# A state-space layer inside a two-block network: within-chunk blocks multiplied in four quadrants and placed by transfers, skip term by TensorE, decay rows by ScalarE

## What is computed

```python
def s5_mixer(h, a_re, a_im, log_dt, b_re, b_im, c_re, c_im, d_skip, w_glu):
    ...                      # ab = exp(a * dt), bb = discretised b, complex
    u = h.reshape(B, S, S5_GROUPS, S5_GROUP)          # 128 groups of 16 channels
    def per_sequence(u_s):
        bu_re = jnp.einsum('sgc,gpc->sgp', u_s, bb_re)
        bu_im = jnp.einsum('sgc,gpc->sgp', u_s, bb_im)
        _, _, x_re, x_im = lax.associative_scan(_scan_combine, (a_seq_re, a_seq_im, bu_re, bu_im), axis=0)
        return jnp.einsum('sgp,gcp->sgc', x_re, cr) - jnp.einsum('sgp,gcp->sgc', x_im, ci)
    y = lax.map(per_sequence, u).reshape(B, S, D)
    y = y + d_skip * h                                # the skip term
    g = jax.nn.gelu(y)
    val, gate = jnp.split(g @ w_glu, 2, axis=-1)
    return val * jax.nn.sigmoid(gate)
```

## Time and profile before

| | us |
|---|---|
| median of 3 runs (2895.97 to 2900.55) | 2896.2 |
| span of the profiled execution, first to last instruction | 2892.0 |
| TensorE busy (19064 matmuls) | 2857.4 |
| VectorE busy | 1879.2 |
| ScalarE busy | 1417.9 |
| GpSimd busy | 393.4 |
| the S5 loop, first `drive` to the first product of `gl0` | 1884.4 to 2000.1 |
| one turn of the loop, by the starts of `drive` | 7.30 |

### The profile page before, as it was taken

One profiled execution on the slowest core, in us unless ns is written; L12 is line 12 of the kernel. 1 busy time (PEld: TensorE's weight loads), 2 busy tenths in 40 slices (PEclk: granted clock), 3 DMA queues, 4 the chain that ended last, 5 costly groups with the idle time before them and its releaser, 6 DMA issues.

```text
span 2892.0 us, 45428 instructions
## 1 busy us (share of the span) xinstructions
PE 2857.4 (99%) x19064; PEld 2606.1 (90%) x19064; DVE 1879.2 (65%) x2575; ACT 1417.9 (49%) x1964; POOL 393.4 (14%) x444
## 2 busy tenths in 40 slices
PE   8999999999999999999999999999999999999998
PEld 8999988998899988989998899898889999988997
DVE  6998655766566655778666666588555555555555
ACT  5445645456455555444444445654545444444444
POOL 0000000000000000008873663043000000000000
PEclk9999999999999999999999999999999999999999
DMA  7555455552555545567776666585655555555553
GB/s 244 190 195 172 155 189 187 188 178 74 187 195 172 171 168 175 193 202 248 238 245 216 231 230 211 186 258 165 204 190 184 195 191 194 198 190 192 197 194 131
DMA packets 288043, 558.45 MB, mean 193 GB/s; under 512 B 27424, under 2 KB 35872, under 8 KB 287584
## 3 DMA queue, kind: packets, MB, share of 16 engines
q1 hardware_dynamic: 281376, 531.27, 55.7%
q0 software_dynamic: 5456, 21.73, 1.9%
q10 hardware_dynamic: 1008, 2.55, 0.3%
HBM read 530.34 MB, written 25.17 MB: 192 GB/s over the span
## 4 chain that ended last, share of the span: by engine, by line
PE 92%; DVE 4%; ACT 2%; issue 1%; POOL 0%; DMA 0%; ACTq 0%; DVEq 0%; POOLq 0%
PE G L506 86%; PE T L506 4%; DVE WL L1648 1%; ACT WH L1071 1%; DVE Y L1656 1%; PE T L585 1%; PE G L979 0%; ACT SC_e L1074 0%; DVE X L1648 0%; DVE ST L1729 0%; DVE SC_e L1656 0%; ACT L1068 0%; POOL ZZ L2428 0%; DMA X<-in_x 0%; PE T L964 0%
## 5 line engine op out<-in xcount | busy, mean ns | idle before, releaser
L1648 DVE TENSOR_TENSOR WL<-RAW,WH 128x1024 fp32r<-128x1024 f32 (+1 forms) x948 | 1183.8, 1258 | 754.7 <-ACT WH L1071 745.3
L1071 ACT ACTIVATE WH<-RAW 128x1024 fp32r<-128x1024 f32 (+1 forms) x948 | 993.8, 1055 | 1027.4 <-PE G L506 1025.5
L506 PE MATMUL G<-A1h,WH 128*128 128x256 f32 (+1 forms) x2583 | 717.9, 279 | 1.6 <-DVE WL L1648 1.6
L506 PE MATMUL G<-A1l,WH 128*128 128x256 f32 x2560 | 710.7, 278 | 0.0
L506 PE MATMUL G<-A1h,WL 128*128 128x256 f32 x2560 | 709.4, 277 | 0.0
L506 PEld LDWEIGHTS G<-A1h,WH 128*128 128x128 f32 x2583 | 485.7, 188 | 5.1 <-DVE WL L1648 2.9
L506 PEld LDWEIGHTS G<-A1l,WH 128*128 128x128 f32 x2560 | 482.3, 188 | 0.4
L506 PEld LDWEIGHTS G<-A1h,WL 128*128 128x128 f32 x2560 | 482.4, 188 | 0.0
L506 PE MATMUL G<-WH,Bh 128*128 128x512 f32 x1024 | 399.3, 390 | 0.6 <-DVE WL L1648 0.6
L506 PE MATMUL G<-WH,Bl 128*128 128x512 f32 x1024 | 398.5, 389 | 0.0
L506 PE MATMUL G<-WL,Bh 128*128 128x512 f32 x1024 | 398.5, 389 | 0.0
(11 more groups left out here) (325 smaller groups left out, 3564.6 us busy)
## 6 DMA issues: line engine op xcount, KB each, us to landing
RAW<-in_mlp_w SPq DMA_DIRECT2D x256, 1024.0 KB, 5.4
RAW<-in_even_w_in SPq DMA_DIRECT2D x52, 1024.0 KB, 5.0
RAW<-in_a_w_in SPq DMA_DIRECT2D x48, 1024.0 KB, 5.2
RAW<-in_b_w_glu SPq DMA_DIRECT2D x32, 1024.0 KB, 5.4
RAW<-in_odd_w_in SPq DMA_DIRECT2D x20, 1024.0 KB, 5.0
RAW<-in_even_w_out SPq DMA_DIRECT2D x16, 1024.0 KB, 5.1
RAW<-in_odd_w_out SPq DMA_DIRECT2D x16, 1024.0 KB, 5.1
RAW<-in_a_w_out SPq DMA_DIRECT2D x16, 1024.0 KB, 5.0
```

What stands on the lines that cost most here:

```text
L506: return e.matmul(out, lhsT, rhs, start=start, stop=stop, skip_group_check=True)
L1071: return e.activation(out, in_, ACT.Copy, scale=scale, bias=0.0)
L1648: return e.tensor_tensor(out, a, b, op)
```

## The change

Five things are changed in the S5 stage.

1. `within` puts the four pairs on the four partition quarters of the bank (rows 32m to 32m+31, columns 0 to 127) and takes the products in another order (i outside, m inside). Four products of 32x32, of the identity with a new matrix DD, add the diagonal of d to the first 32 columns: the skip term is now part of the block.
2. `within` (ACT) makes one copy of 128x128 into KD. SP writes KD to a DRAM tensor (`blocks_out`, 64 KB) and, when that has landed, reads it into FD with four transfers (`blocks_placed`, 64, 48, 32 and 16 KB), which do the shift. `feed` waits for these.
3. `feed` moves one turn later on PE, and behind `within`: the loop is `drive(a)`, `turn_w(a+1)`, `within(a+1)`, `feed(a-1)`, `readout(a-1)`; `feed(15)` and `readout(15)` go into `gl0`.
4. `output` (DVE) is gone, as are DU (POOL) and DST; gelu reads the PSUM bank.
5. The decay rows MG are made by ACT (`decay`, four copies of 128x64 with a scale) instead of by POOL (one product of 128x256).

```diff
@@ pe @@
+            if a == 0:
+                e.wait_ge(*eye["d"])
+            for i in range(2):
+                for m in range(4):
+                    mm(T[32 * m:32 * m + 32, 0:128], W[:, i, m, 96:128], R[:, i, m, 0:128], i == 0, False)
             for m in range(4):
-                for i in range(2):
-                    tk = mm(T[0:32, 128 * m:128 * m + 128], W[:, i, m, 96:128], R[:, i, m, 0:128], i == 0, i == 1)
+                tk = mm(T[32 * m:32 * m + 32, 0:32], IDENT[:, 32 * m:32 * m + 32], DD[:, a, :], False, True)
             tk.then_inc(*f_mm.up(a))
...
         def feed(a):
-            e.wait_ge(*f_c[a])
+            e.wait_ge(*k_back[a % 2][a])
             if a >= 2:
-                e.wait_ge(*y_sum[a - 2])
+                e.wait_ge(*gelu[a - 2])
...
             if 1 <= a < 15:
                 turn_w(a + 1)
-            feed(a)
-            if 1 <= a < 15:
                 within(a + 1)
             if a:
+                feed(a - 1)
                 readout(a - 1)
+        def last_readout():
+            feed(15)
+            readout(15)
@@ act @@
             if a >= 2:
-                e.wait_ge(*fd_mm[a - 2])
-            elif a == 0:
-                e.wait_ge(*zeros["fd"])
-            T = block_bank(a)[0:32, :].rearrange("p (a b) -> p a b", b=128)
-            for j in range(4):
-                c = copy(FD[a % 2][32 * j:32 * j + 32, :, 32 * j:128], T[:, :, 0:128 - 32 * j])
-            c.then_inc(*f_c.up(a))
+                e.wait_ge(*k_out[a % 2][a - 2])
+            copy(KD[a % 2], block_bank(a)[:, 0:128]).then_inc(*f_c.up(a))
+
+        def decay(a):
+            if a >= 2:
+                e.wait_ge(*scan[a - 2])
+            for m in range(4):
+                d = copy(MG[a % 2][:, 64 * m:64 * m + 64], KEEP[:, :], M4[:, 4 * a + m:4 * a + m + 1])
+            d.then_inc(*mg.up(a))
...
-            fn(YG[a % 2], YS[a % 2], ACT.Gelu_apprx_tanh).then_inc(*gelu.up(a))
+            fn(YG[a % 2], G[a % 2][:, 0:256], ACT.Gelu_apprx_tanh).then_inc(*gelu.up(a))
@@ dve @@
-        def output(a):
-            e.wait_ge(*y_mm[a])
-            e.wait_ge(*du[a])
-            if a >= 2:
-                e.wait_ge(*gelu[a - 2])
-            tt(YS[a % 2], G[a % 2][:, 0:256], DU[a % 2], ALU.add).then_inc(*y_sum.up(a))
@@ pool @@
+        tt(DD, EYE.unsqueeze(1).to_broadcast([128, 16, 32]), col("b_d", 0, 16).unsqueeze(2).to_broadcast([128, 16, 32]),
+           ALU.mult).then_inc(*eye.up("d"))
...
-            tt(by_pair(DU[a % 2]), US[:, m, :], DST[:, m].unsqueeze(2).to_broadcast([128, 4, 64]), ALU.mult).then_inc(*du.up(a))
-            if a >= 2:
-                e.wait_ge(*scan[a - 2])
-            tt(MG[a % 2].rearrange("p (a b) -> p a b", b=64), KEEP[:, :].unsqueeze(1).to_broadcast([128, 4, 64]),
-               M4[:, m].unsqueeze(2).to_broadcast([128, 4, 64]), ALU.mult).then_inc(*mg.up(a))
@@ sp @@
+        def blocks_out(a):
+            e.wait_ge(*f_c[a])
+            e.dma_start(KR[a], KD[a % 2]).then_inc(*k_out[a % 2].up(a, 16))
+
+        def blocks_placed(a):
+            e.wait_ge(*k_out[a % 2][a])
+            if a >= 2:
+                e.wait_ge(*fd_mm[a - 2])
+            else:
+                e.wait_ge(*zeros["fd"])
+            v = KR[a].rearrange("(m c) x -> c m x", c=32)
+            for j in range(4):
+                e.dma_start(FD[a % 2][32 * j:32 * j + 32, :, 32 * j:128], v[:, :, 0:128 - 32 * j]).then_inc(
+                    *k_back[a % 2].up(a, 16))
...
             for a in range(20):
+                if 2 <= a < 16:
+                    blocks_placed(a)
                 if a < 14:
                     drive_matrices(a + 2)
                 if a == 0:
                     stacks(3)
+                    blocks_out(0)
+                    blocks_out(1)
+                if a == 1:
+                    blocks_placed(0)
+                    blocks_placed(1)
...
                 if 3 <= a < 19:
                     gelu_out(a - 3)
+                if 1 <= a < 15:
+                    blocks_out(a + 1)
                 if a in (3, 5, 7, 9):
                     load(gl0 + (a - 3) // 2)
```

More of the change, by code:

```diff
@@ L206, in build_program @@
     M4 = sb("M4", [128, 64], ctx=ctxs)
-    DST = sb("DST", [128, 64], ctx=ctxs)
+    sb("pad_dst", [128, 64], ctx=ctxs)
     RBS = sb("RBS", [128, 64], ctx=ctxs)
@@ L222, in build_program @@
     CTD = [VAR5[:, 2048 + 256 * i:2304 + 256 * i].rearrange("p (a b) -> p a b", b=16) for i in range(2)]
-    YS, DU, MG, YG = ([VAR5[:, 512 * n + 256 * i:512 * n + 256 * i + 256] for i in range(2)] for n in range(4))
+    MG, YG = ([VAR5[:, 512 * n + 256 * i:512 * n + 256 * i + 256] for i in range(2)] for n in (2, 3))
+    DD = VAR5[:, 0:512].rearrange("p (a b) -> p a b", b=32)
+    KD = [VAR5[:, 512 + 128 * i:640 + 128 * i] for i in range(2)]
+    EYE = VAR5[:, 768:800]
     YB = [VAR5[:, 2048 + 256 * i:2304 + 256 * i] for i in range(4)]
@@ L234, in build_program @@
     HD = nc.dram_tensor("s5_h", (4, 128, 4, 256), F32, kind="Internal").ap()
+    KR = nc.dram_tensor("s5_k", (16, 128, 128), F32, kind="Internal").ap()
     YD = nc.dram_tensor("s5_y", (16, 4, 32, 4, 64), F32, kind="Internal").ap()
@@ L413, in build_program @@
     u_sc = sig("u_sc")
-    du = sig("du")
+    eye = sig("eye")
+    k_out = [sig(f"k_out{i}") for i in range(2)]
+    k_back = [sig(f"k_back{i}") for i in range(2)]
     mg = sig("mg")
@@ L425, in build_program @@
     y_mm = sig("y_mm")
-    y_sum = sig("y_sum")
     gelu = sig("gelu")
@@ L453, in taken @@
         if tag == "s5_y":
-            return y_sum[14 + i]
+            return gelu[14 + i]
         if tag == "s5_w":
@@ L1045, in pe @@
             gemm(f"gl{i}", A1h, A1l, None if i else (lambda kt: e.wait_ge(*g_low[kt])),
-                 None if i else (lambda: readout(15)), 1)
+                 None if i else last_readout, 1)
             gemm(f"gg{i}", A1h, A1l)
@@ L1565, in act @@
         mlp(0, "s", HT, lambda k: col("norm_mix", 16 + k), first_matrices)
+        e.wait_ge(*zeros["keep"])
+        e.wait_ge(*d_step["m4"])
+        decay(0)
         turned(1)
@@ L1568, in act @@
         for a in range(16):
+            if a < 15:
+                decay(a + 1)
             if a >= 2:
@@ L1584, in act @@
         high_tile(11)
-        e.wait_ge(*fd_mm[15])
+        e.wait_ge(*y_mm[14])
         for _ in range(RS - 2):
@@ L2280, in s5_params @@
             yield
-            for m in range(4):
-                for j in range(4):
-                    e.tensor_copy(DST[32 * j:32 * j + 32, m:64:4], col("b_d", 0, 16)[32 * m:32 * m + 32, :]).then_inc(
-                        *d_step.up("dst"))
-                    yield
         def params():
@@ L2340, in dve @@
         for a in range(16):
-            if a >= 2:
-                output(a - 2)
             chain(a)
@@ L2348, in dve @@
                 low_tile(a - 5)
-        output(14)
         low_tile(11)
@@ L2354, in dve @@
         low_tile(12)
-        output(15)
         low_tile(13)
@@ L2500, in pool @@
             e.dma_start(SPR[a], STR).then_inc(*sp_r.up(a, 16))
+        for m in range(4):
+            if m:
+                e.wait_ge(*eye[m - 1])
+                tt(EYE, EYE, IDENT[:, 32 * m:32 * m + 32], ALU.add).then_inc(*eye.up(m))
+            else:
+                e.tensor_copy(EYE, IDENT[:, 0:32]).then_inc(*eye.up(m))
+        e.wait_ge(*eye[3])
+        tt(DD, EYE.unsqueeze(1).to_broadcast([128, 16, 32]), col("b_d", 0, 16).unsqueeze(2).to_broadcast([128, 16, 32]),
+           ALU.mult).then_inc(*eye.up("d"))
         e.wait_ge(*c_io["c"])
```

6 lines of the change are left out of this document (1 added, 5 removed).

## The result

The changed kernel takes 2925.6 us in the median (2922.5 to 2928.7), the kernel before 2898.4 us beside it on the same chip (2896.0 to 2902.4). The ratio is 1.0094, 95% interval 1.0082 to 1.0105. It is slower, as forecast, and SP's stream sets the pace of the loop, as forecast. But it loses 27 us where 9.6 were worked out, and the time lies above the range of 2892 to 2919. A trace is of one execution, which can be some us from the median of its kernel (this one took 2928.7 us).

The account below looks back on a forecast made before the run. TensorE bounds the kernel before at 7.30 us a turn; after, SP's stream would at 8.8. A loop 8.7 us longer plus 0.9 for `feed(15)` gives +9.6 on the 2896.2 median: 2906 us, range 2892 to 2919.

Parts of the forecast that it names:

- the main case: S5 loop: SP's turn of 8.3 to 9.6 us, L from 3.1 to 4.4, time 2901 to 2914; chance 0.55.
- the sum's own terms: SP's turn from WB to WB: 3.13 + 3.6 + 1.89 + 0.2 = 8.8 us.
- L: In SP's stream, time from issuing `blocks_out` to its landing: taken as 3.6 us, ends 1.6 and 5.6.
- the walk: Step-by-step times through the S5 stage: WB(4) at 1901.1, WB(6) 1916.0, WB(15) 1995.2, `gl0` at 2008.8.
- then `blocks_out(3)` when the copy is there, near 1902: Start of the stage: `blocks_out(3)` issued near 1902, landing 3.6 us later at 1905.6, WB(5) at 1907.6.
- some 5 us: Start of the stage: TensorE stands still for some 5 us before `feed(0)`.
- the sentence on the clock: End of the stage: the kernel before's clock loss there is left as it is, despite TensorE waiting some 2.6 us each turn.
- The short round trip: Rival in SP's loop: `blocks_out` lands at L = 2.0 or less, turn 7.2 us, about 2889 us; chance 0.15.
- The quarters do overlap: Against the rival in `within` of no overlap: up to 2.8 us instead of 0.8, time 2908; chance 0.08.
- The rival of the clock: Rival in the loop: waits bring TensorE to 1.2 GHz for part of every turn, turn 9.3 us, 2914; chance 0.17.
- ScalarE's decay copies cost nothing: Loop: ACT's decay copies ahead of `turned`, which might hold `drive`, priced at nothing because `scan[a-1]` is done earlier.

Follow-up runs that it names:

- the run with the filled wait: Changed kernel plus twelve unread identity products (36 in the first turn) between `drive` and `turn_w`, to hold TensorE's clock up; 2928.1 us, ratio 1.0109.
- the transfer by ScalarE: Changed kernel with `blocks_out` issued by ScalarE right behind its copy to KD, placements still by SP; 2908.3 us, ratio 1.0040.
- RD behind: Changed kernel with the load of the readout matrices (RD) issued behind the blocks' transfer to `s_k`, not ahead of it; 2922.2 us, ratio 1.0079.
- both orders: Changed kernel with placements issued behind the four GELU-tile writes and the RD load behind the blocks' transfer to `s_k`; 2912.4 us, ratio 1.0045.

## Why the prediction was right in kind and wrong in size

**TensorE's part was right.** 6.2 us a turn forecast, 6.12 measured; `within` and the identity 0.8, measured 0.46 + 0.18 = 0.64.

**That SP's stream would bound the loop was right**, and the place of the wait too. The turn was 9.69 us instead of 8.8, just above the 9.6 at which the main case ended. Over the nine turns from WB(6) to WB(15), by the sum's own terms:

| term | forecast | measured (mean) |
|---|---|---|
| WB, RD, read and four writes, to `blocks_out` | 3.13 | 3.72 |
| L, `blocks_out` to its landing | 3.6 | 3.91 |
| placements, to the next WB | 1.89 | 2.06 |
| the 1 MB load | 0.2 | 0, it lies inside L |

The term most mis-sized is the first, the issues: I had taken their price from single turns of the kernel before. In the changed loop four writes take 1.85 to 2.81 us (2.13 in the turn above) and four placements up to 2.76. I take it that the queue accepts more slowly when more is under way; no run isolates that. 9 x 0.89 = 8.0 us. L was a good guess, though by rows that did not quite say it: the 3.4 us of the earlier trace rows is the median of all 61 writes, not of those behind a RD load. In the nine turns L is 2.5 to 5.3. In the three turns that hold a 1 MB load it is 2.5 to 3.5 and the turn some 9 us; in the turn behind each of them it is 4.4 to 5.3 and the turn some 11. The last two turns alternate in the same way without a load (8.46 and 9.89), so the load is not all of it.

**The start was wrong by 6 us**: WB(6) at 1921.98, not 1916.0. Up to WB(4) the walk holds (1901.1 forecast, 1901.65 measured). The step that failed is the next, "then `blocks_out(3)` when the copy is there, near 1902". It came at 1909.48, and SP waited 6.1 us for the copy. TensorE shows why:

```profile
1897.66 1.97 PE L511 MATMUL G<-US,FD 128*128 128x64 f32 x8 [7.85 <-DMA FD<-s_k]
1899.42 3.62 PE L511 MATMUL G<-ZZ,RD 128*128 128x63 f32 x16
1902.84 3.62 PE L511 MATMUL T<-US,LAM 128*128 128x64 f32 x16
1906.25 1.91 PE L984 MATMUL G<-CID,WB 128*128 128x128 f32 x8
1908.09 0.90 PE L511 MATMUL T<-RD,WB 128*32 128x128 f32 x16
```

I had forecast "some 5 us" of standing still; it was 7.85. And behind it the clock was at half: from this `feed` to `within` 1908.09 - 1897.66 = 10.4 us, where the same four steps take 0.94 + 1.79 + 1.79 + 0.97 = 5.5 in the turn shown first. These 5 us are nearly all of the six. I had followed SP's stream to 1902 and not the chain on TensorE that the copy hangs on: even at full clock `within` would have started at 1903.2 and `blocks_out(3)` near 1904.5. That the rest would be won back at full clock is read from these rows and from the run with the filled wait (5.5 us there too, without its filler), which made the start longer by other means. A shorter wait alone does not do it: without the long wait (the first block's round trip moved before the start), and without any transfer, the same steps took 10.4 and 10.5 us.

**The end was wrong by 7 us**: 20.6 us from WB(15) to `gl0`, not 13.6.

```profile
2013.03 1.09 PE L984 MATMUL G<-CID,WB 128*128 128x128 f32 x8 [1.95 <-DMA WB<-s_w]
2014.99 1.08 PE L511 MATMUL T<-RD,WB 128*32 128x128 f32 x16 [0.87 <-issue]
...
2017.88 3.62 PE L511 MATMUL G<-ZZ,RD 128*128 128x63 f32 x16
2021.29 3.62 PE L511 MATMUL T<-US,WT 128*128 128x64 f32 x16
```

At full clock it is 13.7 (the run with the filled wait), which is the forecast. The step that failed is the sentence on the clock: "I leave this loss in the end of the stage as it is". The rows at 1992 had shown the loss for a short stretch; here everything behind the last `turn_w` runs at half speed: 14.8 us from `within` (2014.99) to `gl0`, where it is 7.9 in the run with the filled wait (2016.40 to 2024.27).

**Sum**: forecast 8.7, start 6.0, turns 8.0, end 7.0: 29.7 us, and `gl0` begins at 2029.79 instead of 2000.06, 29.7 later. `feed(15)` inside `gl0` and a longer stretch at half clock there add 2.1 (0.9 forecast). The profiled executions are 34.8 us apart. The last 3 us come behind a wait of 2.78 us for DVE that both have, some 185 us after the start of `gl0`: in the changed kernel it is followed by half clock, in the kernel before by full clock. As far as the traces tell this does not belong to the change: in three more kernels with the same code from there on (the transfer by ScalarE, RD behind, both orders) the mean clock of the 20 us around this wait was 0.91, 1.00 and 0.91, where it is 0.83 and 1.00 in the two compared. The medians are only 27.2 apart, since the trace of the changed kernel is of an execution above its median (2928.7 us, 2925.6) and that of the kernel before of one below its median (a span of 2892.0; 2898.4). So the account is one of the two traces; for the medians it is 7.6 us too long, and no trace says which of its terms are smaller there.

**The rivals.** The short round trip did not come: L was 3.9, not 2.0. The quarters do overlap. The rival of the clock happened, but together with the main case and in another place than I had put it. I had weighed it only by whether TensorE's turn would pass SP's; in the loop it did not matter (9.61 and 9.69). It mattered where TensorE itself is on the path: at the start, where SP waits for it, and at the end, where nothing but TensorE is left. Treating the two as exclusive made the range too narrow: main case plus clock was the case to price. That ScalarE's decay copies cost nothing was right.

**The fixed cost.** With nothing of size ahead of it `s_k` landed after 1.6 us, in the loop after 3.9 in the mean. The Trainium skill, "DMA: Bandwidth & Descriptors", section Anatomy of one DMA, gives for a DMA by GpSimd's path a fixed cost of about 2.0 us plus the bytes. These transfers go by SP's queue: with 1.6 us the first landed somewhat sooner than that; with 3.9 us the others took nearly twice as long.

## What to carry over

A transfer with a wait for its landing in the same in-order queue costs its time to landing in every turn, whatever the engines have to spare. In a queue that also feeds the next turn, the place of the transfers matters much (2896.9 to 2925.6 us in the orders tried here), but none of these orders beat the kernel before beyond its interval. A small on-chip copy may look dear per element (0.24 us for 32x32 to 32x128) and still be cheaper than a round trip through DRAM: sixteen of them, in the right place in ScalarE's order, gave 2887.0 us. When a forecast puts a wait of two or three microseconds into TensorE's stream, price what follows it at half clock as well, and look first at the places where TensorE's chain is on the path: the first turn and the last.

## What the runs showed of the hardware

- Sixteen fp32 matmuls of 128x128 on 32 columns each took 1.86 us on one quarter of the columns and 0.46 us when neighbours in the order went to four different quarters.
- TensorE's granted clock went to the lower level (1.2 GHz) behind waits of 2.06, 2.70 and 1.43 us in a loop with a turn of 9 to 11 us, and stayed there for about a turn (0.50 to 0.52 in windows in which the engine was busy all the time). A wait of 2.78 us elsewhere was followed by it in some traces and not in others.
- A 64 KB write landed after 1.6 us at the quietest and 5.3 us at the latest in one stage; issuing four placements took 1.74 us at one time and 3.43 us at another in one kernel (the one with both orders).
